# State of the delta scan in a two-layer hybrid block: whole 128x128 tiles in place of 64x64 quarters

## The reference, cut to what matters

```python
def step(s, xs):
    u_n, w_n, k_n, gl_n = xs
    v_new = u_n - w_n @ s
    s_next = s * jnp.exp(gl_n)[..., None, None] + jnp.einsum("bhcd,bhce->bhde", k_n, v_new)
    return s_next, (s, v_new)

s_final, (s_prev, v_new) = lax.scan(step, s0, (u, w, k_dec, g_last))
o = jnp.einsum("nbhcd,nbhde->nbhce", qc * jnp.exp(G)[..., None], s_prev) + qk @ v_new
```

## Time and profile before

| | |
|---|---|
| Device time, median of 3 runs | 2490.29 us (2488.69 to 2491.06) |
| The profiled execution's own time | 2489.88 us |
| Its span, first to last instruction | 2487.7 us |
| PE busy | 2297.3 us (92%), 16570 instructions |
| PE weight load busy | 1890.4 us (76%) |
| DVE busy | 1470.8 us (59%), 2156 instructions |
| ACT busy | 1121.1 us (45%) |
| POOL busy | 111.7 us (4%) |
| Mean granted clock of TensorE | 0.958 of full speed |

### The profile page before, as it was taken

One profiled execution on the slowest core, in us unless ns is written; L12 is line 12 of the kernel. 1 busy time (PEld: TensorE's weight loads), 2 busy tenths in 40 slices (PEclk: granted clock), 3 DMA queues, 4 the chain that ended last, 5 costly groups with the idle time before them and its releaser, 6 DMA issues.

```text
span 2487.7 us, 39471 instructions
## 1 busy us (share of the span) xinstructions
PE 2297.3 (92%) x16570; PEld 1890.4 (76%) x16570; DVE 1470.8 (59%) x2156; ACT 1121.1 (45%) x1545; POOL 111.7 (4%) x90
## 2 busy tenths in 40 slices
PE   6998989799998999895978979969999999999997
PEld 4777778677787888784766969958888888888885
DVE  2134767433334222334456664439999999899997
ACT  3224331222223222224244024228778787787785
POOL 0000440000000000000004300000000000000000
PEclk9998999899999999997989979969999999999998
DMA  8882001322103222220300045319899898998994
GB/s 323 332 333 91 1 3 71 119 96 90 68 34 140 102 87 100 85 87 34 102 1 1 4 170 175 114 68 347 338 350 363 342 364 344 350 358 340 349 362 171
DMA packets 63331, 448.40 MB, mean 180 GB/s; under 512 B 7216, under 2 KB 8240, under 8 KB 9520
## 3 DMA queue, kind: packets, MB, share of 16 engines
q1 hardware_dynamic: 60880, 434.86, 46.3%
q10 hardware_dynamic: 2272, 10.97, 1.2%
HBM read 443.71 MB, written 2.10 MB: 179 GB/s over the span
## 4 chain that ended last, share of the span: by engine, by line
PE 86%; DVE 6%; ACT 4%; issue 2%; DMA 1%; POOL 1%; PEld 0%; ACTq 0%; SPq 0%; DVEq 0%; PEldq 0%; POOLq 0%
PE bank L1100 11%; PE bank L1190 10%; PE bank L616 9%; PE bank L597 7%; PE bank L599 7%; PE bank L598 6%; PE bank L1201 5%; PE bank L977 5%; PE bank L702 3%; PE bank L1126 3%; PE bank L1109 3%; PE bank L470 3%; PE bank L757 3%; PE bank L714 2%; PE bank L634 2%
## 5 line engine op out<-in xcount | busy, mean ns | idle before, releaser
L1921 DVE TENSOR_TENSOR wsp_l<-ring,wsp_h 128x1024 fp32r<-128x1024 f32 x528 | 640.1, 1224 | 38.6 <-ACT wsp_h L1283 8.1
L1283 ACT CAST wsp_h<-ring 128x1024 fp32r<-128x1024 f32 x528 | 555.4, 1054 | 142.9 <-PE bank L599 86.8
L597 PE MATMUL bank<-wsp_h,xTs_h 128*128 128x512 f32 x704 | 283.8, 403 | 3.7 <-DVE wsp_l L1921 3.7
L599 PE MATMUL bank<-wsp_h,xTs_l 128*128 128x512 f32 x704 | 276.3, 393 | 0.0
L598 PE MATMUL bank<-wsp_l,xTs_h 128*128 128x512 f32 x704 | 275.2, 391 | 0.0
L2428 DVE TENSOR_TENSOR dsp_l<-ring,dsp_h 128x1024 fp32r<-128x1024 f32 x66 | 80.8, 1225 | 243.4 <-ACT dsp_h L1659 243.4
L2366 DVE TENSOR_TENSOR gsp_l<-ring,gsp_h 128x1024 fp32r<-128x1024 f32 x64 | 78.2, 1225 | 190.9 <-ACT gsp_h L1608 190.6
L1100 PE MATMUL bank<-u_hi,gsp_h 128*128 128x512 f32 (+1 forms) x512 | 184.0, 359 | 6.8 <-DVE gsp_l L2366 6.8
L1659 ACT CAST dsp_h<-ring 128x1024 fp32r<-128x1024 f32 x66 | 69.0, 1047 | 259.6 <-PE bank L1190 177.7
L1100 PE MATMUL bank<-u_hi,gsp_l 128*128 128x512 f32 (+1 forms) x512 | 174.4, 341 | 0.0
L1100 PE MATMUL bank<-x_lo,gsp_h 128*128 128x512 f32 (+1 forms) x512 | 174.3, 341 | 0.0
(11 more groups left out here) (334 smaller groups left out, 4471.4 us busy)
## 6 DMA issues: line engine op xcount, KB each, us to landing
ring<-in_moe_tiles_dram SPq DMA_DIRECT2D x264, 1024.0 KB, 4.8
ring<-in_ada_tiles_dram SPq DMA_DIRECT2D x48, 1024.0 KB, 11.0
ring<-in_ffn_tiles_dram SPq DMA_DIRECT2D x33, 1024.0 KB, 4.8
ring<-in_gate_tiles_dram SPq DMA_DIRECT2D x32, 1024.0 KB, 4.9
ring<-in_in_tiles_dram SPq DMA_DIRECT2D x22, 1024.0 KB, 4.9
arena<-in_branch_tiles_dram ACTq DMA_DIRECT2D x8, 1024.0 KB, 5.8
ring<-in_out_tiles_dram SPq DMA_DIRECT2D x8, 1024.0 KB, 4.8
halfc<-in_halfc_dram SPq DMA_DIRECT2D x1, 1040.0 KB, 18.0
```

Of the source, the lines that this page charges most:

```text
L597: pe.matmul(o, xTs[0][:, kk, :], whi[:, k, :], start=(kk == 0), stop=False)
L599: mm = pe.matmul(o, xTs[1][:, kk, :], whi[:, k, :], start=False, stop=(kk == KD - 1))
L1283: act.copy(wsp[0][:, g % 4, :], half_slot(MOE0, g)).then_inc(s.gq_o.up, 1)
L1921: v.tensor_tensor(wsp[1][:, g % 4, :], half_slot(MOE0, g), wsp[0][:, g % 4, :], ALU.subtract).then_inc(s.gq_pt.up, 1)
```

## The change

The state is updated as whole 128x128 tiles. PE writes the products of a pair of heads to the places in bank `2 + dr` that the blocks have in the tile, so that the bank holds a 128x128 matrix with two blocks on the diagonal for each pair `a`. The quarters off the diagonal in banks 2 and 3 are set to zero once for each layer, after `u` has been copied from the bank, by two memsets for each bank. The copy, the memsets and the signal are linked, so DVE waits twice on itself for each of the two banks. The matmuls of the scan write only the blocks on the diagonal. In step 0 one copy of 128x256 for each direction takes the place of four copies of 64x64, and in steps 1 to 6 two fused operations of 128x128 for each direction take the place of four of 64x64.

```diff
                             for a in range(2):
                                 for hp in range(2):
                                     hh = 2 * a + hp
-                                    mm = pe.matmul(bank[2 + dr][rows[hp], CH * a:CH * (a + 1)], kdec[dr][rows[c], t, CH * hh:CH * (hh + 1)],
+                                    mm = pe.matmul(bank[2 + dr][rows[hp], P * a + CH * hp:P * a + CH * (hp + 1)], kdec[dr][rows[c], t, CH * hh:CH * (hh + 1)],
                                                    vnew[rows[c], 2 * dr + hp, 2 * t + a, :], start=True, stop=True)
...
                 for g in range(4):
                     v.wait_ge(*s.u_mm(g + 1))
-                    v.tensor_copy(vnew[:, g].rearrange("p x n -> p (x n)"), bank[g][:, :]).then_inc(s.u_ok.up, 1)
+                    ins = v.tensor_copy(vnew[:, g].rearrange("p x n -> p (x n)"), bank[g][:, :])
+                    if g >= 2:
+                        link(ins)
+                        for hp in range(2):
+                            at = CH * (1 - hp)
+                            ins = v.memset(bank[g][rows[hp], 0:BW].rearrange("p (a n) -> p a n", a=2)[:, :, at:at + CH], 0.0)
+                        link(ins)
+                        v.sem_inc(s.u_ok.up, 1)
+                    else:
+                        ins.then_inc(s.u_ok.up, 1)
...
                             v.wait_ge(*s.st_s(2 * i + dr + 1))
-                            for a in range(2):
-                                for hp in range(2):
-                                    part = slice(CH * hp, CH * (hp + 1))
-                                    x, upd = S[part, dr, a, part], bank[2 + dr][part, CH * a:CH * (a + 1)]
-                                    if i == 0:
-                                        ins = v.tensor_copy(x, upd)
-                                    else:
-                                        at = 2 * dr + a
-                                        ins = v.scalar_tensor_tensor(x, x, decay_to[part, k % 2, k // 2, at:at + 1], upd,
-                                                                     ALU.mult, ALU.add)
+                            if i == 0:
+                                ins = v.tensor_copy(S[:, dr].rearrange("p a n -> p (a n)"), bank[2 + dr][:, 0:BW])
+                            else:
+                                for a in range(2):
+                                    at = 2 * dr + a
+                                    ins = v.scalar_tensor_tensor(S[:, dr, a, :], S[:, dr, a, :],
+                                                                 decay_to[:, k % 2, k // 2, at:at + 1],
+                                                                 bank[2 + dr][:, P * a:P * (a + 1)], ALU.mult, ALU.add)
                             ins.then_inc(s.st_S.up, 1)
```

## The result

| | before | after |
|---|---|---|
| Device time, median of 4 runs each | 2490.68 us (2488.69 to 2493.81) | 2474.40 us (2470.34 to 2475.49) |
| The profiled execution | 2489.88 us | 2470.34 us |
| Scan of layer 0, first update to L2338 (now L2345) | 28.8 us | 21.7 us |
| Scan of layer 1 | 29.7 us | 19.7 us |

The ratio of the means is 0.9929 (95% interval 0.9917 to 0.9941), and the medians differ by 16.3 us. The forecast was 11.05 us off, 2479.2 us, with a range down to 2475.5. The profiled execution is the fastest of its four, so its spans differ by more than the medians: 2487.7 to 2468.5, or 19.2 us.

What follows compares the result with a forecast made beforehand. DVE's state update was taken to bound the two scans, with PE close behind and bounding them after the change. Layer 0's 4.85 and layer 1's 6.20 sum to 11.05 us off 2490.29, giving 2479.2 us, range 2475.5 to 2483.5.

Steps and rivals of the forecast that it cites:

- The slower rival: Rival, DVE's wide updates: each costs 745 ns, every step 0.62 us longer, 2497.7 us in all; chance 0.03.
- PE is already the bound: Rival, scan steps with output matmuls: PE's busy 3.53 us cannot be compressed, gain 8.45, 2481.8 us; chance 0.13.
- Direction 1 follows 0.96 later: Scan step on PE: direction 1's `w @ S` starts 0.96 us behind direction 0's, at 1.76, though its state is ready at 1.13.
- The new step: Forecast's paragraph on a scan step after the change: PE's order sets the period, 3.27 us instead of 3.92 in step 1.
- forecast 4.85 off: Scan of layer 0: the savings of steps 0 to 6 together, 4.85 us.
- the 3.27: Period in us forecast for a scan step with output matmuls, first update to next update, set by PE's order.
- the rival that I gave 0.20: Rival, layer 1's scan: the clock never falls, steps 1 and 2 take 2.45 us each, 2477.5 us; chance 0.20.
- my cases: The forecast, chance 0.42, and its four rivals, chances 0.22 (clock in layer 1 as now, 2480.5 us), 0.20, 0.13 and 0.03.

Runs made afterwards that it cites:

- the filler: Kernel before, with four matmuls of constants on PE behind L1070 in steps 0, 1 and 2 of layer 1: 2489.70 us, ratio 0.9986.
- the padded kernel: Changed kernel with a 512-column memset of an unused tile on DVE between the two directions' updates in each updating step: 2477.93 us, ratio 0.9950.
- the last experiment: Changed kernel with the second output parts (L1078) behind both state products only in steps 0, 1, 4 and 5: 2475.40 us, ratio 0.9938.
- Late outputs: Changed kernel with both second output parts (L1078) moved behind both state products (L1070) in PE's list: 2472.74 us, ratio 0.9921.

## Why the prediction was wrong in size

**What held.** The reading that DVE's update bounded the scan and PE was close behind held: the update is gone from the chain, PE is busy throughout in the steps with outputs, and the gain lies in the two scans. The estimate for the wide operation (346 ns, four in 1.13 us) measured 344 ns and 1.15. The memsets and links are covered, as taken (at most 0.1 us in sight, 1.0006 by experiment), but with nothing to spare, which was luck: the forecast's own bounds for them went up to 1.0 us in each layer. PE's start behind the update (0.80 forecast, 0.87 measured), the 1.02 to L1070 and the 0.49 to the next update held. Step 0 of layer 1 was forecast at 2.60 and took 2.55. Behind the scans nothing caught up. The slower rival and "PE is already the bound" are out: PE's busy 3.53 us of a step did shrink, to 2.88.

**The step that failed** is the sentence "Direction 1 follows 0.96 later" in "The new step". I took the 0.96 us between the two directions' L1052 in step 0 of the earlier trace rows (417.69 to 418.65) for the time that one direction's L1052 and L1059 take PE to issue. It was not PE's time. DVE's eight narrow copies were the reason, which these rows of the timeline of the kernel before show:

```profile
416.71 1.89 DVE L2319 COPY S<-bank 64x64 f32<-64x64 f32 x8 [2.90 <-PE bank L1070]
...
418.07 0.47 PEld L1059 LDWEIGHTS bank<-S,ring 128*64 128x64 f32 x4
```

PE's loads for direction 0 were through at 418.54 (418.07 + 0.47). The copies ended at 418.60 (416.71 + 1.89), and PE took direction 1 at 418.65, as soon as its state was there. In the changed kernel, with both states ready, the gap is 0.49, because the directions write different halves and run side by side. With the same half for both it is 0.82, and the step 3.26. So a step with outputs takes 2.88, not 3.27:

- layer 0: forecast 4.85 off, 7.1 measured, or 2.25 more;
- layer 1, steps 4 to 6: about 1.2 more; step 3, which ends with the first `q @ S`, against the 3.27 forecast: 2.70, or 0.57 more.

That is 4.0 of the 6.0 us by which the scans gave more than forecast (17.05 against 11.05).

**The second miss is the rival that I gave 0.20**, that the clock never falls. Steps 1 and 2 of layer 1 took 2.32 each, where I forecast 3.29 at the low clock: 1.9 us more, which with the 4.0 makes up the 6.0. The rival's own estimate was 2.45. I took the fall from the step 0 before it (PE busy 1.68 of 3.02 us), but in the changed kernel PE was busy 1.25 of 2.55 in that step, no larger a share, and the clock stayed. That the shorter steps 1 and 2 keep it up fits the filler (narrow updates, more work on PE: a later fall) and the padded kernel (wide updates, longer steps: a fall), but each is one profile, and the clock fell in the last experiment as well, after a step 0 no different from the others'. So the pauses as the reason are argued and not shown. What is shown is the count: it fell in four of four profiles with narrow updates and no filler, and in one of eight with wide ones, leaving out the 512-column memset.

The rest, 2.2 us of the span outside the scans, was forecast as chance (1.5 either way for each layer); 1.5 of it are the first gate groups. The range was too narrow because both of its ends used the 3.27: in my cases the step with outputs had that length or more, and none had PE issue the two directions any faster.

**What stays open.** What makes the single "issue" gaps in PE's list is not known. They took 0.3 to 1.7 us, sat mostly ahead of step 0 and in step 2 of layer 0 (3.35, 3.08, 2.88, 3.49 and 3.76 us for that step in five profiles), and differ between profiles of one kernel. In three of these the profile puts the pause in step 2 down to DVE's update, but that direction's state had been ready for 0.7 us or more. What exactly lets the clock fall, in layer 1 or in step 0 of layer 0, is not known either. Late outputs save 0.19 us in steps 1 and 5 and lose 0.43 at the end of the scan, and their time could not be told from that of the changed kernel.

## What to carry to other kernels

An interval between two groups of one engine's rows is that engine's own price only if nothing else could have ended there: before using it as a bound, look at what the other engine finished just ahead of it, and take the interval from a place where both inputs had long been ready. When a stage is bound by many small fused operations, first make them whole tiles, even where half of a tile is zeros; here twice the columns cost 64 ns an operation and halved the count. And where the granted clock falls in a stage with pauses of TensorE, a change that shortens them can have a second gain behind the first one, which deserves a larger chance than the 0.20 that it had here.

## What the runs showed of the hardware

- Two chains of 128x64 loads that write different halves are issued between each other, 0.49 us apart; on the same half they are 0.82 apart, and a step of the scan takes 3.26 instead of 2.88 us.
- Eight fused 64x64 operations from PSUM take 2.36 us when their start partition alternates at every one, 1.97 when at every second one, or about 0.1 us for each change. Four of 128x128, all from partition 0, take 1.15.
- At a change from 128x64 to 64x64 weights PE's list shows a gap of 0.17 us that no semaphore ends, in all four timelines quoted above; at the change back there are 0.07 (421.99 to 422.06). An order with twice as many such changes, and a wait of 0.31 us for the subtraction, took 0.15 us a step more.
- With wide updates the granted clock went from 1.00 to 0.56 in layer 1 after a step with PE busy 2.08 of 2.74 us, and stayed at 1.00 after one with 2.00 of 2.32. In the one other profile with wide updates where it fell there, step 1 ran at 0.50 after a step 0 like the others' (PE busy 1.24 of 2.54), and the steps 1 and 2 took 0.7 to 0.8 us more (3.10 and 3.03 against 2.32).
- In step 0 of layer 0 the granted clock was 0.60 in two profiles with wide updates and a memset between them, and the step took 4.23 us instead of 2.68.
